# A state-space layer run in chunks of four tokens, with its matrices made beside the MLP before it and parked in DRAM

## The reference, cut to what matters

```python
dt = exp(log_dt); mag = exp(lam_re * dt)                 # 128 groups x 64 states
ab = mag * (cos(lam_im * dt) + i sin(lam_im * dt))       # state decay, complex
bb = coef(ab, lam) * b                                   # drive, 64 states x 16 channels a group
x[t] = ab * x[t-1] + bb u[t]                             # u = rmsnorm(x), scan over 256 tokens
y[t] = Re(c x[t]) + d * u[t]                             # readout and skip
g = gelu(y);  val, gate = split(g @ w_glu);  out = val * sigmoid(gate)
```

## Time and profile before

| | us |
|---|---|
| median of 3 runs | 3191.51 |
| profiled execution, own time | 3190.09 |
| its span | 3188.3 |
| first MLP to its last product, end | about 1969 |
| S5 stage, 1976.00 to first matmul of `gg0` at | 2306.08 |

### The profile page before, as it was taken

The page is one execution under the profiler, slowest core; times in us unless marked ns, Lnnn a source line. Parts: engine busy times, 40 slices in busy tenths (PEclk is TensorE's granted clock), DMA queues, the critical chain, the costliest instruction groups (busy, mean ns, idle before and its releaser), DMA issues.

```text
span 3188.3 us, 44953 instructions
## 1 busy us (share of the span) xinstructions
PE 3035.1 (95%) x18832; PEld 2644.0 (83%) x18832; DVE 2034.1 (64%) x2953; ACT 1517.7 (48%) x2193; POOL 9.0 (0%) x16
## 2 busy tenths in 40 slices
PE   8999999998999999999999998888899999999998
PEld 8988888987899988999999996333387999999996
DVE  5996655844655566855555555999855555555555
ACT  5335545444544454444444445666544444444443
POOL 0000000000000000000000000000000000000000
PEclk9999999999999999999999998899999999999999
DMA  6555355523545555565555553000065555555553
GB/s 233 172 185 172 133 194 175 164 74 121 187 163 169 170 172 183 189 198 194 189 189 194 186 191 125 1 14 14 30 217 176 194 183 198 193 186 192 190 186 131
DMA packets 257370, 512.38 MB, mean 161 GB/s; under 512 B 8128, under 2 KB 12352, under 8 KB 256912
## 3 DMA queue, kind: packets, MB, share of 16 engines
q1 hardware_dynamic: 255584, 504.00, 47.5%
q0 software_dynamic: 864, 2.95, 0.3%
q10 hardware_dynamic: 720, 2.55, 0.2%
HBM read 507.37 MB, written 2.10 MB: 160 GB/s over the span
## 4 chain that ended last, share of the span: by engine, by line
PE 77%; DVE 17%; ACT 3%; issue 2%; DMA 1%; SPq 0%; ACTq 0%; DVEq 0%
PE G L413 73%; DVE WL L1427 4%; DVE Y L1435 3%; PE T L413 3%; DVE XX L1427 2%; DVE WW L1427 2%; DVE ZZ L2049 1%; ACT WH L911 1%; DVE ZZ L1427 1%; PE T L463 1%; DVE TW L1435 1%; DVE HT L1427 0%; DVE ST L1502 0%; ACT Z L914 0%; ACT T L914 0%
## 5 line engine op out<-in xcount | busy, mean ns | idle before, releaser
L1427 DVE TENSOR_TENSOR WL<-RAW,WH 128x1024 fp32r<-128x1024 f32 (+1 forms) x940 | 1140.7, 1221 | 856.4 <-ACT WH L911 844.7
L911 ACT ACTIVATE WH<-RAW 128x1024 fp32r<-128x1024 f32 (+1 forms) x940 | 985.5, 1055 | 1105.3 <-PE G L413 1096.5
L413 PE MATMUL G<-A1h,WH 128*128 128x256 f32 x2560 | 723.3, 283 | 8.7 <-DVE WL L1427 8.6
L413 PE MATMUL G<-A1l,WH 128*128 128x256 f32 x2560 | 716.3, 280 | 0.0
L413 PE MATMUL G<-A1h,WL 128*128 128x256 f32 x2560 | 716.2, 280 | 0.0
L413 PEld LDWEIGHTS G<-A1h,WH 128*128 128x128 f32 x2560 | 485.9, 190 | 11.2 <-DVE WL L1427 10.4
L413 PEld LDWEIGHTS G<-A1h,WL 128*128 128x128 f32 x2560 | 487.8, 191 | 0.0
L413 PEld LDWEIGHTS G<-A1l,WH 128*128 128x128 f32 x2560 | 485.1, 189 | 0.8
L413 PE MATMUL G<-WH,Bh 128*128 128x512 f32 x1024 | 398.9, 390 | 0.0
L413 PE MATMUL G<-WH,Bl 128*128 128x512 f32 x1024 | 398.4, 389 | 0.0
L413 PE MATMUL G<-WL,Bh 128*128 128x512 f32 x1024 | 398.4, 389 | 0.0
(11 more groups left out here) (284 smaller groups left out, 3735.4 us busy)
## 6 DMA issues: line engine op xcount, KB each, us to landing
RAW<-in_mlp_w SPq DMA_DIRECT2D x256, 1024.0 KB, 5.2
RAW<-in_even_w_in SPq DMA_DIRECT2D x56, 1024.0 KB, 5.2
RAW<-in_a_w_in SPq DMA_DIRECT2D x48, 1024.0 KB, 5.1
RAW<-in_b_w_glu SPq DMA_DIRECT2D x32, 1024.0 KB, 5.4
RAW<-in_odd_w_in SPq DMA_DIRECT2D x20, 1024.0 KB, 4.9
RAW<-in_even_w_out SPq DMA_DIRECT2D x16, 1024.0 KB, 5.1
RAW<-in_odd_w_out SPq DMA_DIRECT2D x16, 1024.0 KB, 5.1
RAW<-in_a_w_out SPq DMA_DIRECT2D x16, 1024.0 KB, 5.0
```

The source lines that it names most:

```text
L413: return e.matmul(out, lhsT, rhs, start=start, stop=stop, skip_group_check=True)
L911: return e.activation(out, in_, ACT.Copy, scale=scale, bias=0.0)
L1427: return e.tensor_tensor(out, a, b, op)
```

## The change

The state-space layer works on chunks of four tokens. For each group of four channel tiles `a` (16 of them, 4 pairs of groups `m` in each) the state exists at 64 chunk ends instead of 256 tokens, so that one round on VectorE covers four of the former tiles. Its matrices for drive (`STW`) and for readout and inner products (`STR`) are computed by GpSimd during the first MLP and written to two DRAM tensors, 0.5 MB and 0.625 MB for each `a`; SP reads them back as the stage runs (`WB`, `RD`). `within` multiplies the two to get the matrix inside the chunk (`FD`), `turn_w` transposes the drive matrices. All angle tables (`TC`, `TS`) are made during the first MLP, 64 by 64 a partition. `gl0` becomes an ordinary split product after the stage, and its splits wait until the stage is over, since the stage's tiles `WT`, `FD` and `WW` lie on `WH` and one of `RD` on `WL`. GpSimd also scales the inputs (`inputs`) and sums the turned states (`x_sum`); ScalarE makes the GELU.

```diff
-        weights(f"gl{i}", t["b_w_glu_2"][0], 2048, 512 * i, steps=1, split=i > 0)
+        weights(f"gl{i}", t["b_w_glu_2"][0], 2048, 512 * i, steps=1)
...
+    C_STEPS = (110, 130, 150, 170)
...
+        def turn_c():                         # pe, beside the first MLP
+            for n in range(171):
+                if n in C_STEPS:
+                    q = C_STEPS.index(n)
+                    e.wait_ge(*p_gen["cd", q])
...
+                    for i in range(2):
+                        for c in range(4):
+                            m = e.transpose(TB[2 + i][:, 128 * c:128 * c + 128], CDQ[i][:, c, :], IDENT)
+                    m.then_inc(*c_t.up(q))
+                yield
...
+        def turn_w(a):
+            e.wait_ge(*w_back[a % 2][a])
...
+            for i in range(2):
+                for m in range(4):
+                    tk = e.transpose(G[2 + i][:, 128 * m:128 * m + 128], WB[a % 2][:, i, m, 0:128], IDENT)
+            tk.then_inc(*wt_t.up(a))
+
+        def within(a):
...
+            e.wait_ge(*r_back[a % 3][a])
...
+            for m in range(4):
+                for j in range(4):
+                    for i in range(2):
+                        tk = mm(T[:, 128 * m + 32 * j:128 * m + 32 * j + 32], W[:, i, m, 96 - 32 * j:224 - 32 * j],
+                                R[:, i, m, 0:32], i == 0, i == 1)
+            tk.then_inc(*f_mm.up(a))
+
+        def drive(a):
...
+            for i in range(2):
+                for m in range(4):
+                    tk = mm(T[:, 256 * i + 64 * m:256 * i + 64 * m + 64], WT[a % 2][:, i, m, :], US[:, 4 * a + m, :],
+                            True, True)
...
+        def feed(a):
...
+            for m in range(4):
+                tk = mm(G[a % 2][:, 64 * m:64 * m + 64], FD[a % 2][:, m, :], US[:, 4 * a + m, :], m == 0, False)
...
+        def readout(a):
+            e.wait_ge(*x_sum[a])
+            for m in range(4):
+                for i in range(2):
+                    tk = mm(G[a % 2][:, 64 * m + 1:64 * m + 64], RD[a % 3][:, i, m, 32:160], XS[a % 2][:, i, m, 0:63],
+                            False, i == 1)
...
+        turn_w(0)
+        within(0)
+        rows("s", TB[1])
+        for a in range(17):
+            if a < 16:
+                drive(a)
+                feed(a)
+            if a < 15:
+                turn_w(a + 1)
+                within(a + 1)
+            if a:
+                readout(a - 1)
...
+                if n >= 215 and n % 5 == 0 and n < 235:   # act, beside the first MLP
+                    tables((n - 215) // 5)
...
+        def chain(a):                         # dve: the eight operations of a tile, on four tiles' chunks
...
+        for a in range(18):
+            if a >= 2:
+                output(a - 2)
+            if a < 16:
+                chain(a)
+            if a in (9, 13, 17):
+                low_tiles((a - 9) // 4)
+            if a == 16:
+                limit[0] = len(halves)
+                for _ in range(RS):
+                    split_next()
...
+        for a in range(16):                   # pool, beside the first MLP
+            m = slice(4 * a, 4 * a + 4)
...
+            products(BB[0][:, m, :], BB[1][:, m, :], 0, 4 * a)
...
+            sums(STW, (ALU.subtract, ALU.add)).then_inc(*p_gen.up(("w", a)))
...
+            e.dma_start(SPW[a], STW).then_inc(*sp_w.up(a, 16))
...
+        def matrices(a):                      # sp
...
+            e.dma_start(WB[a % 2][:, :, :, 0:128], SPW[a]).then_inc(*w_back[a % 2].up(a, 16))
+            if a >= 3:
+                e.wait_ge(*y_mm[a - 3])
...
+            e.wait_ge(*sp_r[a])
+            e.dma_start(RD[a % 3][:, :, :, :], SPR[a]).then_inc(*r_back[a % 3].up(a, 16))
```

More of the change, by code:

```diff
@@ L821, in drive @@
[L821 to L876, removed]
+        def turn_c():
[3 more added lines that the diff above has]
+                    e.wait_ge(*p_gen["cd", q])
+                    if q:
+                        e.wait_ge(*c_c[q - 1])
+                    for i in range(2):
[3 more added lines that the diff above has]
+                yield
@@ L1381, in act, with turned, within @@
-        limit[0] = len(halves)
-        e.wait_ge(*g_low[7])
-        e.wait_ge(*raw_read[first_chunk["gl0"] + 3])
+        def turned(a):
+            e.wait_ge(*wt_t[a])
+            if a >= 2:
+                e.wait_ge(*b_mm[a - 2])
+            for i in range(2):
+                c = copy(WT[a % 2][:, i, :, :], G[2 + i][:, :].rearrange("p (a b) -> p a b", b=128))
+            c.then_inc(*wt_c.up(a))
+        def within(a):
+            e.wait_ge(*f_mm[a])
+            if a >= 2:
+                e.wait_ge(*fd_mm[a - 2])
+            copy(FD[a % 2][:, :, :], TB[2 + a % 2][:, :].rearrange("p (a b) -> p a b", b=128)).then_inc(*f_c.up(a))
@@ new lines, in act @@
+        turned(0)
+        within(0)
+        for a in range(17):
+            if a < 15:
+                turned(a + 1)
+                within(a + 1)
+            if a < 8:
+                stack_last(a // 2, 2 * (a % 2))
+                stack_last(a // 2, 2 * (a % 2) + 1)
+            if a >= 5:
+                gelus((a - 5) // 4, (a - 5) % 4)
+        limit[0] = len(halves)
+        e.wait_ge(*fd_mm[15])
+        e.wait_ge(*scan[15])
+        for _ in range(RS):
+            split_next()
@@ new lines, in tt, with products @@
+        def tt(out, a, b, op):
+            return e.tensor_tensor(out, a, b, op)
+        def products(x, y, at, m0):
+            lam = [LAM[:, i, at:at + 4, m0:m0 + 4].rearrange("p a b -> p b a").unsqueeze(3).to_broadcast([128, 4, 4, 16])
+                   for i in range(2)]
+            x, y = (v.unsqueeze(2).to_broadcast([128, 4, 4, 16]) for v in (x, y))
+            tt(TP[0], x, lam[0], ALU.mult)
+            tt(TP[1], y, lam[1], ALU.mult)
+            tt(TP[2], x, lam[1], ALU.mult)
+            tt(TP[3], y, lam[0], ALU.mult).then_inc(*p_gen.up("p"))
+            e.wait_ge(*p_gen["p"])
@@ new lines, in sums @@
+        def sums(out, ops):
+            for g in range(2):
+                ps, cs = slice(64 * g, 64 * g + 64), slice(16 * g, 16 * g + 16)
+                for i in range(2):
+                    d = tt(out[ps, i, :, :].rearrange("p a (b c) -> p a b c", c=32)[:, :, :, cs],
+                           TP[2 * i][ps], TP[2 * i + 1][ps], ops[i])
+            return d
+        e.memset(STW, 0.0).then_inc(*zeros.up("st"))
+        e.memset(KEEP[:, :], 1.0).then_inc(*zeros.up("st"))
+        e.wait_ge(*zeros["st"])
@@ new lines, in pool @@
+        masked(0)
+        for a in range(16):
+            q, m = a // 4, slice(4 * (a % 4), 4 * (a % 4) + 4)
+            if a % 4 == 0:
+                e.wait_ge(*c_c[q])
+                if q < 3:
+                    masked(q + 1)
+            if a:
+                e.wait_ge(*p_gen["r", a - 1])
+            else:
+                e.wait_ge(*p_gen["w", 15])
+            if a:
+                e.wait_ge(*sp_r[a - 1])
+            for i in range(2):
+                e.tensor_copy(STR[:, i, :, 0:32], CTM[i][:, m, :])
+            products(CTD[0][:, m, :], CTD[1][:, m, :], 4, 4 * a)
+            sums(STR[:, :, :, 32:160], (ALU.add, ALU.subtract)).then_inc(*p_gen.up(("r", a)))
+            e.wait_ge(*p_gen["r", a])
+            e.dma_start(SPR[a], STR).then_inc(*sp_r.up(a, 16))
```

555 lines of the change are left out of this document (330 added, 225 removed).

## The result

The changed kernel takes 3293.51 us (median of 4 runs, 3290.74 to 3302.31) against 3192.16 us for the kernel before (median of 4): a ratio of 1.0326, with a 95% interval of 1.030 to 1.0352. Forecast were 3280 us and 1.028. The profiled execution took 3290.74 us with a span of 3288.9, against 3190.09 and 3188.3: 100.6 us more, where the sum had 89.6.

A forecast was written before the change was run, and what follows sets the result against it. TensorE was taken to bound the first MLP and, once changed, the stage, where VectorE had set the pace. From the profiled 3190.1 us, +80.1 (stage), +3.5 (transposes) and +6 (MLP stalls) gave 3279.7, predicted as 3280; range 3095 to 3315.

The forecast's parts named there:

- the low clock: State-space stage: TensorE at 1.2 GHz throughout, total 3280 us, own range 3250 to 3315, chance 0.56.
- Where the kernel before is slow: Reading of the old profile: TensorE busy and at full clock almost everywhere except slices 26 to 29, the state-space stage.
- Clock: State-space stage: few streamed columns, nearest row at clock 0.51, so 1.2 GHz taken for the whole stage.
- full-clock rival: Stage: loads keep 2.4 GHz or do not slow at 1.2, rounds 13.0 us, total 3106 us; chance 0.25.
- Round: Stage: TensorE's 104 records and 8 transposes take 24.0 us a round at 1.2 GHz, 13.0 at 2.4 GHz.
- Path of the stage: From the norm's transposes through `drive(0)`, 15 rounds of 24.0 us and a newly exposed `gl0`: `gg0` 80.1 us later.
- First MLP: `tables` bursts on ScalarE delay weight copies: 1 to 2 us show, four times, 6 us in all (0 to 16).
- The cover: First MLP: four halves are 10.9 us of TensorE's work, so a pause of 7.2 us behind a `tables` burst is covered.
- The cover of GpSimd's work: First MLP: 44 operations and 4 DMAs a quarter in 54.8 us, so up to 1.2 us an operation is hidden.
- third rival: GpSimd late in the first MLP, TensorE standing at `turn_c`: 140 us more, 3420 us at half clock; chance 0.07.
- VectorE's burst: First MLP: some 22 dependent operations of 0.3 us for the powers of the decay, said to fit at no cost.
- Transposes of `turn_c`: First MLP: 32 transposes added to TensorE, the bound engine, at 0.108 us each, 3.5 us.

The follow-up runs named there:

- wide128: The kernel after, with each matmul of `within` streaming up to 128 columns of `RD` instead of 32, same loads: 3137.55 us, ratio 0.982 to the kernel before.
- wide_mlp_split: The kernel after with four edits in the first MLP, `within` streaming `RD`'s 32 columns repeated up to four times, and `RD` read back in two parts: 3103.74 us.
- the four like executions: Profiled executions of the kernel after, wide64, wide128 and loads_cut, all with the same program in the first MLP: 755.0, 752.3, 748.2 and 748.7 us there.
- wide64: The kernel after, with each matmul of `within` streaming up to 64 columns of `RD` instead of 32, same loads: 3247.1 us.
- loads_cut: The kernel after, with `within` loading only the 32, 64, 96 or 128 weight columns that can be nonzero, and `FD` copied accordingly: 3247.39 us.
- wide96_cut: wide_mlp_split with the loads of `within` cut as in loads_cut and 96 streamed columns instead of 128: 3109.58 us.

## Why the prediction came out as it did

The sign, the place and the mechanism were right. The total, 11 us short of the profiled difference, is closer than its parts: the MLP was 25 us too low and the start 3 us, the stage 17 us too high. That they nearly cancel is luck. So is something of the hit itself: the low clock had a chance of 0.56, and the range of 3095 to 3315 had to hold both signs.

- **Where the kernel before is slow.** The prediction puts the stage in slices 26 to 29 with an 8 in the clock. In the earlier trace rows the eights of PE are slices 25 to 29, and the clock has an 8 in 25 and 26 alone. Nothing in the sum hangs on it; the windows of the earlier trace rows carry it.
- **Clock.** Taken as 1.2 GHz for the whole stage, by the nearest row; measured 0.52. Shown by wide128: with more columns behind the same loads it is 1.00. The chance of 0.25 for the full-clock rival was for its mechanism, that loads keep the clock up; they don't. Its price, 3106, was 32 us too low for wide128 (3137.55), 18 of them in the MLP (27.9 us over the kernel before, where 9.5 was taken); that wide_mlp_split has 3103.74 is no match of like with like, since it lacks the wait for the readback and most of the MLP's loss, which the price has in it.
- **Round.** 24.0 forecast, 23.79 measured; a record 0.213, as forecast; loads of 128 columns 333 ns (330). At 2.4 GHz 12.3 plus 0.7 for `RD`; measured 12.44 without that wait and 13.23 with it.
- **Path of the stage.** `drive(0)` 16.9 us behind the norm's transposes (16.6), 15 rounds in 340.9 us (360.0), from `drive(15)` to `gl0` 15.3 (14.3), `gl0` 25.3 (24.4). The 19 us too many in the rounds: the first one has no readout (3.5), four short returns of the clock (12.4), and 15 times 0.21. That round 0 reads nothing out stands in the loop, and the step overlooked it; the returns are not the same in every execution, and the step left them out.
- **First MLP, the step that failed.** `tables` was put at 6 us, and 13.6 was measured alone (9.7 against the mean of the four like executions). The burst's length was right. The cover was enough for two of the four bursts and not for the first and the third; their two pauses, 3.9 and 3.7 us, are 7.6 together, not far above the 6. What the sum had at nothing is the half clock behind the pauses: three stretches of 3.4 us by the granted clock, which cost 5.1 us. Why the cover fails behind two bursts was not tested.
- **The cover of GpSimd's work.** "Up to 1.2 us an operation is hidden" counted operations and no waits. In the MLP its products take 894 to 1038 ns in the mean and its sums 1049 to 1066 (0.7 was taken, 612 to 727 in the stage), and it waited 66.7 us in 15 turns for its own writes of `STR`, 0.6 to 8.0 a turn. The last quarter took 58.1 us (1701.6 to 1759.7), one wait of 7.2 in it, against the 54.8 that `C_STEPS` left: a small form of the third rival, 4 to 8 us instead of 140.
- **Costed at nothing.** VectorE's burst was said to fit; the 16 copies into `DST` took 9.6 us between the `WL` of a few halves, and 16 stacking copies sat ahead of the addition that the norm waits for: 4.0 (with what the edits share) and 3.6 us.
- **Transposes of `turn_c`.** 3.5 forecast, 3.8 measured (from the first of 8 to the next load three times 1.00 us and once 0.86).

What stays open: why the kernel after's clock returns for a short while in some rounds and not in others, and why one write of `STR` takes twice as long to land in some executions. The 2.9 us ahead of the first MLP are no effect of the change as far as the traces can tell: the ten variants of the kernel after, whose program is the same up to there, reach that place between 1249.8 and 1256.1 us, and the kernel before, at 1250.6, lies among them.

## What to carry to other kernels

Where TensorE's pace is set by weight loads, look at the granted clock before counting anything else: a stage that streams little behind wide loads can run every load at half speed, and columns that are streamed for nothing, as long as they take no longer than the load, bring it back; here 128 did, and 64 behind full loads only late. Cut the loads to the columns that hold something, but change their size as rarely as possible. A cover is counted in the time of the helper's whole loop, its waits for its own transfers included, and a pause of the bound engine costs its length and the slow work behind it.

## What the runs showed of the hardware

- Loads go by the column and by the clock: 128 columns every 0.213 us at 1.2 GHz, 0.112 at 2.4 GHz (`within` in 7.15 us). The Trainium skill ("TensorE: Matmul & The Clock Gate", LDWEIGHTS) gives 107 ns for 128 columns and names no clock. At 2.4 GHz the trace nearly agrees; for 1.2 GHz the measurement decides.
- The same loop can hold either level of the clock for 100 us or more (wide64).
- Behind a change of the load's width the first load comes 0.17 to 0.19 us late at 1.2 GHz (loads_cut) and 0.17 at 2.4 GHz (wide96_cut), except from 96 to 128 columns.
- VectorE and GpSimd slow each other. The split of the weights, 1370 to 1700 us, after and then before:

```profile
L1502 DVE TENSOR_TENSOR WL<-RAW,WH 128x1024 fp32r<-128x1024 f32 x117 | 157.1, 1351 | 118.2 <-ACT WH L977 117.2
```

```profile
L1427 DVE TENSOR_TENSOR WL<-RAW,WH 128x1024 fp32r<-128x1024 f32 x119 | 145.0, 1225 | 134.5 <-ACT WH L911 132.4
```

The same operation takes 10% more in the mean. Sorted by what GpSimd does meanwhile, the records of the kernel after show where that comes from: the 42 with no operation of GpSimd beside them take 1225 ns in the mean and 1226 at most, as in the kernel before; the 56 that lie to over 80% beside one take 1453 ns, 1210 to 1806. The other way round, GpSimd's products (`TS<-VAR,LAM`) take 634 to 652 ns with nothing on VectorE (17 records), and 1079 in the mean, up to 1704, where VectorE works for more than half of their time (37).
